# Column quarters for two modulation weights, and the order of slots and late units in a two-block kernel

## What is computed

```python
mod_x = (silu(c) @ w_mod + b_mod)          # 6 x 1024: sh1, sc1, g1, sh2, sc2, g2
mod_c = silu(c_ctx) @ w_mod + b_mod        # the same weights for a second vector
x   = x + g1x * (attention(...) @ w_out)
hx2 = rmsnorm(x) * (1 + sc2x) + sh2x
x   = x + g2x * peer(hx2)                  # g2x: the last two of twelve slices of w_mod

def peer(h):                               # rows in chunks of 128
    q = (h @ w_q).reshape(C, 8, 2, 128)
    s = einsum('chpd,hpnd->chpn', q, subkeys)
    sv, si = top_k(s, 16)                  # 16 per half; then 16 of the 256 pairs: ids
    a = gelu(einsum('cd,chkd->chk', h, u[ids]))
    return einsum('chk,chkd->cd', softmax(best) * a, v[ids])
```

## Time and profile before

| | us |
|---|---|
| median of 3 runs (lowest, highest) | 1465.23 (1464.28, 1466.23) |
| the profiled execution | 1464.12 |
| its span, first to last instruction | 1462.2 |
| busy PE, DVE, ACT, POOL | 1324.0, 1108.5, 629.8, 318.4 |
| gathers (268.45 of 416.32 MB) | share of 16 DMA engines 44.4% |
| mean granted clock of PE | 0.967 |

### The profile page before, as it was taken

How to read it: one execution, slowest core, us unless ns; L and a number is a source line. 1 busy time by engine, 2 the same in 40 slices (tenths; PEclk the granted TensorE clock), 3 DMA queues, 4 the chain that set the end, 5 groups by cost and what they waited for, 6 DMA issues and landing times.

```text
span 1462.2 us, 16525 instructions
## 1 busy us (share of the span) xinstructions
PE 1324.0 (91%) x5512; PEld 874.0 (60%) x5512; DVE 1108.5 (76%) x2315; ACT 629.8 (43%) x1322; POOL 318.4 (22%) x307
## 2 busy tenths in 40 slices
PE   9998899998797978697897799999999999999998
PEld 3876664543343424253343346678888877788887
DVE  6688857867776776766677777879998577799974
ACT  5343733223221222222221225567776445677752
POOL 0000003544444444344444430000110000011100
PEclk9999999999898989899898899999999999999999
DMA  9624457999999999999999996434545434345530
GB/s 392 270 116 192 160 248 308 421 422 422 420 422 421 422 422 420 422 417 421 418 421 410 413 413 264 171 118 156 190 173 198 156 117 166 115 179 198 199 144 30
DMA packets 50437, 416.32 MB, mean 285 GB/s; under 512 B 5552, under 2 KB 5680, under 8 KB 7088
## 3 DMA queue, kind: packets, MB, share of 16 engines
q0 software_dynamic: 36864, 268.45, 44.4%
q1 hardware_dynamic: 13488, 146.82, 26.3%
HBM read 414.20 MB, written 1.05 MB: 284 GB/s over the span
## 4 chain that ended last, share of the span: by engine, by line
DVE 38%; PE 35%; DMA 15%; issue 6%; ACT 3%; POOL 2%; DVEq 0%; SPq 0%; POOLq 0%; ACTq 0%
DVE arena_r L592 8%; DMA ring<-in_uv,ids 8%; PE ps L1199 6%; DMA arena<-in_uv,ids 6%; DVE ring L2237 4%; PE ps L1278 4%; PE ps L1280 4%; PE ps L1279 4%; DVE arena L2513 4%; DVE arena L2237 3%; DVE arena L2505 2%; DVE arena L2515 2%; PE ps L1018 2%; PE ps L907 2%; PE ps L909 2%
## 5 line engine op out<-in xcount | busy, mean ns | idle before, releaser
L1199 PE MATMUL ps<-ring,arena 128*128 128x512 f32 x632 | 295.2, 617 | 52.2 <-ACT arena L1714 52.2
L2237 DVE CUSTOM_DVE_ANT_0 ring<-ring,arena 128x1024 f32<-128x1024 f32 x158 | 190.5, 1224 | 88.6 <-DMA ring<-in_uv,ids 88.0
L1199 PEld LDWEIGHTS ps<-ring,arena 128*128 128x128 f32 x632 | 122.4, 197 | 215.0 <-issue 142.3
L1486 PE MATMUL ps<-hpair,arena_r 128*128 128x512 f32 x704 | 244.3, 394 | 0.0
L793 POOL DMA_INDIRECT ring<-in_uv,ids x158 | 177.9, 1126 | 228.1 <-PE ps L1199 176.2
L1199 PE MATMUL ps<-arena 128*128 128x512 f32 x392 | 186.1, 621 | 45.0 <-ACT arena L1714 45.0
L592 DVE TENSOR_TENSOR arena_r<-ring,arena_r 128x1024 fp32r<-128x1024 f32 x152 | 185.4, 1223 | 54.3 <-ACT arena_r L577 50.6
L1488 PE MATMUL ps<-hpair,arena_r 128*128 128x256 f32 x704 | 195.0, 277 | 0.0
L577 ACT ACTIVATE arena_r<-ring 128x1024 fp32r<-128x1024 f32 x152 | 158.7, 1053 | 59.0 <-PE ps L1280 58.0
L793 POOL DMA_INDIRECT arena<-in_uv,ids x98 | 105.1, 1072 | 350.5 <-issue 247.8
L1199 PEld LDWEIGHTS ps<-arena 128*128 128x128 f32 x392 | 76.7, 199 | 147.1 <-issue 91.1
(11 more groups left out here) (337 smaller groups left out, 2048.7 us busy)
## 6 DMA issues: line engine op xcount, KB each, us to landing
ring<-in_lw SPq DMA_DIRECT2D x39, 2048.0 KB, 7.9
ring<-in_b1w SPq DMA_DIRECT2D x14, 2048.0 KB, 8.8
ring<-in_b1w SPq DMA_DIRECT2D x9, 1024.0 KB, 16.8
ring<-in_lw SPq DMA_DIRECT2D x8, 1024.0 KB, 5.0
wqb<-in_wq SPq DMA_DIRECT2D x4, 1024.0 KB, 9.0
arena<-in_wq SPq DMA_DIRECT2D x3, 1024.0 KB, 13.5
ring<-in_uv,ids POOLq DMA_INDIRECT x158
ring<-in_lw SPq DMA_DIRECT2D x2, 1088.0 KB, 10.0
```

The lines of the kernel that those rows point to most:

```text
L1199: last = nc.tensor.matmul(ps[:, 4 + 2 * c + b, :], diag[:, k % 4, :], vrows[place(n, k)][:, b * 512:(b + 1) * 512], start=False, stop=(clo ...
L1486: nc.tensor.matmul(ps[:, bank, :].rearrange("p (t n) -> p t n", t=2), high_of(l, p)[:, cols_], hpair[:, :, k, :], start=(k == 0), stop=Fal ...
L2237: V.tensor_tensor_reduce(out=urows[at], in0=urows[at], in1=hrow[:, c, :], scale=1.0, scalar=0.0, op0=ALU.mult, op1=ALU.add, accum_out=dots ...
```

## The change

The last two modulation weights use four column quarters of the array: `sil32` holds the two silu columns and 30 zero columns, product k goes to partitions 32(k mod 4) on, and the eight products become two in each quarter. The copy out takes 128 rows, and `mod_cols` adds the quarters by multiplying with `sum4` (identity of two, repeated). Both weights move on PE from behind the output sums to behind the second key sums of chunk 0 (in place of two steps of `out_sums`, which are spread), and so do their copies on ACT and their bias on DVE. In the attention, turn(15), values(14) and values(15) go behind all output sums of unit 15; values(15) writes into another bank. On ACT, act_pt(15) goes before act_rows(14), and `roots(1, 4)` before the third `heads_in`. Gathers begin with slots 11, 12, 4, 5, 6, 7, 3, 0, 1, 2, 13, 14, 15, and the order changes by swaps of neighbours from round to round until it is the old one; the last nine gathers have their old slots.

```diff
--- before
+++ after
@@ -40,6 +40,7 @@
...
 MOD_A = 4
+MOD_ROWS = 32
 MODA_ORDER = (0, 2, 1, 3)
...
@@ -90,15 +91,37 @@
...
+FIRST_SLOTS = (11, 12, 4, 5, 6, 7, 3, 0, 1, 2, 13, 14, 15)
+def slot_order(count):
+    now, order = list(FIRST_SLOTS), []
+    while len(order) < count:
+        order += now
+        for i in range(len(order) // len(SLOTS) % 2, len(SLOTS) - 1, 2):
+            if SLOTS.index(now[i]) > SLOTS.index(now[i + 1]):
+                now[i], now[i + 1] = now[i + 1], now[i]
+    return order[:count]
+ORDER = slot_order(TOPK * STAGES)
+LAST_USE, TURN, USED_UP_TO = {}, [], []
+for g, at in enumerate(ORDER):
+    TURN.append(ORDER[:g + 1].count(at))
+    USED_UP_TO.append(LAST_USE.get(at, 0))
+    LAST_USE[at] = g + 1
+assert tuple(ORDER[-9:]) == SLOTS[0:9]
 def place(n, k):
-    return SLOTS[(TOPK * n + k) % len(SLOTS)]
+    return ORDER[TOPK * n + k]
 def turn_of(n, k):
-    return (TOPK * n + k) // len(SLOTS) + 1
-LAST_USE = {at: g + 1 for g in range(TOPK * STAGES) for at in (SLOTS[g % len(SLOTS)],)}
+    return TURN[TOPK * n + k]
 ENDS = tuple(GROUP * (g + 1) for g in range(GROUPS))
...
@@ -126,6 +149,7 @@
...
 TURN_BANK = 4
+LAST_VALUES = 3
 MODB_UNIT = (0, 2, 6, 9, 12)
...
@@ -297,6 +321,7 @@
...
         sil2 = small(8, 4)
+        sil32 = rot[:, 0:2, :].rearrange("p a b -> p (a b)").rearrange("p (k m) -> p k m", k=KD)
         modc = small(48, 2)
...
@@ -450,7 +475,7 @@
...
             if i >= MOD_A + MOD_B:
-                return modrow_c[0:2, :]
+                return modrow_c
             return modrow[0:4, i % 2, :]
...
@@ -662,7 +687,7 @@
...
             act.wait_ge(pv_done, m + 1)
-            src = ps[:, 6, 256 * (m % 2):256 * (m % 2) + P]
+            src = ps[:, LAST_VALUES if m == 15 else 6, 256 * (m % 2):256 * (m % 2) + P]
             if t < DIFF:
...
@@ -783,6 +808,7 @@
...
             nc.gpsimd.memset(sil2[:, :, 2:4], 0.0).then_inc(fills, 1)
+            nc.gpsimd.memset(sil32[:, :, 2:MOD_ROWS], 0.0).then_inc(fills, 1)
             nc.gpsimd.memset(zero, 0.0).then_inc(fills, 1)
...
@@ -800,8 +826,8 @@
...
                     pool.wait_ge(ids_ready, 1)
-                if k >= len(SLOTS):
-                    pool.wait_ge(pair_free, NS + k - len(SLOTS) + 1)
+                if USED_UP_TO[k]:
+                    pool.wait_ge(pair_free, NS + USED_UP_TO[k])
                 elif at == 3:
...
@@ -815,7 +841,7 @@
...
                 for k in range(TOPK):
-                    pool.wait_ge(pair_free, NS + TOPK * n + k - len(SLOTS) + 1)
+                    pool.wait_ge(pair_free, NS + USED_UP_TO[TOPK * n + k])
                     gather(n, n % NC, k)
...
@@ -839,8 +865,9 @@
...
                 for k in range(KD):
-                    last = nc.tensor.matmul(ps[0:2, bank, :], sil2[:, k, 0:2], slot(n)[:, k, :],
-                                            start=(k == 0), stop=(k == KD - 1))
+                    rows = slice((k % 4) * MOD_ROWS, (k % 4 + 1) * MOD_ROWS)
+                    last = nc.tensor.matmul(ps[rows, bank, :], sil32[:, k, :], slot(n)[:, k, :],
+                                            start=(k < 4), stop=(k >= 4), skip_group_check=True)
                 last.then_inc(mod_used, 1)
...
@@ -848,7 +875,7 @@
...
                     last = nc.tensor.matmul(ps[:, bank, at + 2 * jj:at + 2 * jj + 2], mod_row(i)[:, jj * P:(jj + 1) * P],
-                                            con("sum4")[0:4, :] if i < MOD_A else ident[0:2, 0:2], start=True, stop=True)
+                                            con("sum4")[0:4 if i < MOD_A else P, :], start=True, stop=True)
                 last.then_inc(modcol_done, 1)
...
@@ -911,7 +938,7 @@
...
-            pe.wait_ge(fills, 3)
+            pe.wait_ge(fills, 4)
             running(3, 8)
...
@@ -993,7 +1020,7 @@
...
                     for kc in range(4):
-                        last = nc.tensor.matmul(ps[:, 6, at:at + P], PT[:, m % 2, 0, kc * P:(kc + 1) * P],
+                        last = nc.tensor.matmul(ps[:, LAST_VALUES if m == 15 else 6, at:at + P], PT[:, m % 2, 0, kc * P:(kc + 1) * P],
                                                 vrow[:, kc, t * P:(t + 1) * P], start=(kc == 0), stop=(kc == 3))
...
@@ -1030,8 +1057,9 @@
...
                     scores(m + 2)
-                turn(m)
-                if m >= 1:
+                if m < 15:
+                    turn(m)
+                if 1 <= m < 15:
                     values(m - 1)
...
@@ -1058,12 +1086,10 @@
...
                     out_sums(1, 5, 4, 5, 6, 7)
+            turn(15)
+            values(14)
             values(15)
             turned(1, range(4, KD), 4)
-            pe.wait_ge(exp_done, 32)
-            pe.wait_ge(o_out, 3)
-            out_sums(0, 2, 0, 1)
...
@@ -1134,11 +1160,21 @@
...
             first_query(1, 7, range(3, KD)).then_inc(first_q, 1)
-            out_sums(0, 2, 2)
+            pe.wait_ge(exp_done, 32)
+            pe.wait_ge(o_out, 3)
+            out_sums(0, 2, 0)
             first_keys(1, 5)
-            out_sums(0, 2, 3)
+            out_sums(0, 2, 1)
+            pe.wait_ge(silu_ready, 2)
+            mod_rows(MOD_A + MOD_B, 6)
             back_to_rows(0, (0, 7))
-            out_sums(1, 3, 0, 1, 2, 3)
+            mod_rows(MOD_A + MOD_B + 1, 4)
+            out_sums(0, 2, 2, 3)
+            pe.wait_ge(row_out, 2)
+            mod_cols(MOD_A + MOD_B, 7)
+            out_sums(1, 3, 0, 1)
+            mod_cols(MOD_A + MOD_B + 1, 7, 8)
+            out_sums(1, 3, 2, 3)
...
@@ -1148,7 +1184,6 @@
...
             out_sums(1, 3, 4, 5, 6, 7)
-            mod_rows(MOD_A + MOD_B, 6)
             norm2_tiles(1, (0, 2))
...
@@ -1156,9 +1191,6 @@
...
             back_to_rows(1, (0, 2))
-            pe.wait_ge(row_out, 2)
-            mod_cols(MOD_A + MOD_B, 7)
-            mod_rows(MOD_A + MOD_B + 1, 6)
...
@@ -1204,11 +1236,10 @@
...
             all_queries(1)
-            mod_cols(MOD_A + MOD_B + 1, 3)
             experts(0, 0, places=range(GROUP, 2 * GROUP))
...
             experts(0, 0, places=range(2 * GROUP, TOPK))
-            pe.wait_ge(mod_out, MOD_A + MOD_B + 1)
+            pe.wait_ge(mod_out, MODS)
             cleared(6, 7)
...
@@ -1536,7 +1567,7 @@
...
                     act.wait_ge(modcol_done, i - 1)
-                nc.scalar.activation(mod_row(i), ps[0:4 if i < MOD_A else 2, bank, :], ACT.Copy).then_inc(modrow_out, 1)
+                nc.scalar.activation(mod_row(i), ps[0:4 if i < MOD_A else P, bank, :], ACT.Copy).then_inc(modrow_out, 1)
...
@@ -1643,11 +1674,10 @@
...
             table(ACT.Sqrt)
+            act_pt(act, 15)
             act_rows(act, 14)
-            act_pt(act, 15)
             act_rows(act, 15)
+            roots(1, 4)
             heads_in(3, range(4, KD), 4)
...
@@ -1678,19 +1708,19 @@
...
-            roots(1, 4)
             norm2_in(0)
...
                 nc.scalar.activation(qTs[:, s, 0:P], ps[:, bank, 0:P], ACT.Copy).then_inc(first_q_out, 1)
+            mod_row_out(MOD_A + MOD_B, 6)
             rows_in(0, (0, 7))
+            mod_row_out(MOD_A + MOD_B + 1, 4)
             heads_in(4, range(4), 0, con("subg"))
...
             table(ACT.Gelu)
-            mod_row_out(MOD_A + MOD_B, 6)
             norm2_in(1)
...
@@ -1717,7 +1747,6 @@
...
             table(ACT.Gelu)
-            mod_row_out(MOD_A + MOD_B + 1, 6)
             query_out(1)
...
@@ -1937,6 +1966,7 @@
...
             V.tensor_copy(sil4[:, :, 0:2], sil2[:, :, 0:2]).then_inc(sil4_ready, 1)
+            V.tensor_copy(sil32[:, :, 0:2], sil2[:, :, 0:2]).then_inc(silu_ready, 1)
             dve.wait_ge(sil4_ready, 1)
...
@@ -2261,13 +2291,14 @@
...
             topk(1, 0, 1)
+            dve.wait_ge(modcol_done, MODS)
             mod_bias(MOD_A + MOD_B, 7)
+            mod_bias(MOD_A + MOD_B + 1, 7, 8)
             for k in range(GROUP, TOPK):
...
             weights(0, 0, 3, ENDS)
-            mod_bias(MOD_A + MOD_B + 1, 3)
             dve.wait_ge(row_out, 4)
...
```

## The result

| | before | after |
|---|---|---|
| median, us (lowest, highest; 22 runs each, side by side) | 1466.45 (1464.28, 1471.43) | 1469.28 (1466.47, 1474.09) |
| ratio, 95% interval | | 1.0020 [1.0014, 1.0027] |
| the profiled execution, us | 1464.12 | 1472.42 |
| its span, us | 1462.2 | 1470.6 |
| last gather issued, us | 861.45 | 866.8 |

The change makes the kernel 2.8 us (0.2%) slower. The forecast was 2.5 us faster, and 1469.28 lies above its range. Up to the first load of the second block (880.15 before, 885.53 after) they are 5.4 us apart; the other 3.0 lie in the second block, which the change does not touch: there the mean of 704 products of one line is 399 ns instead of 394.

What follows compares the result with a forecast made beforehand. Bound by the expert gather stream: 1.3 us from an earlier start plus 1.4 to 2.4 of start loss is 2.7 to 3.7, capped at the 18th gather, so 2.5 us taken: 1462.7 us, range 1460.2 to 1466.5.

Steps and rivals of the forecast that it cites:

- Bound by the gather stream: 256 expert gathers run at the DMA ceiling, 410 to 422 GB/s; only their start, start loss and dry spells count.
- Part 1, late unit: Late attention unit: turn(15) and values(14) go behind the output sums, so everything to the first indices comes 1.33 us sooner.
- rival D: Does nothing: PE's clock falls in the new 1.7 us wait, or slot order or chunk 1 takes the gain; 0.11.
- Part 2, column quarters: Modulation weights on PE: four quarters overlap, 1.9 to 2.2 us a weight instead of 7.03.
- Rivals B and C: Quarters overlap in pairs only, 1464.2 us, chance 0.12; or don't overlap, 1471 us, chance 0.09.
- Part 3, the new order: PE's list: last output sum 236.3, 6.0 us later; chunk 1 turned 3.6 us later, PE's loss repaid behind its indices.
- The 18th gather gains 0.7 to 1.7 us, no more.: Release of the 18th gather: fourth dot ends at 265 to 266, instead of the gelu of 266.98.
- Part 4, gathers: Gather start: six go out at once, nothing runs dry, start loss falls from 3.3 to 0.9 to 1.9 us.
- the cushion of 1.6 us: Data still unmoved when the 18th gather's can begin in the kernel before: 0.68 MB, 1.6 us from dry.
- the 22 early reuses: Cases reusing a slot after 12 gathers instead of 13; 45th and 61st singled out, cost 0, at worst 2 us.
- Rival E: Slower: chunk 1 makes the 18th gather 2 us later and the stream dry there; 3 us lost, 1468.2 us; 0.06.
- The cap by the cushion: At the 18th gather: cushion 1.6 plus 0.7 to 1.7 us sooner limits the gain to 2.3 to 3.3 us.

Runs made afterwards that it cites:

- e1: The changed kernel unaltered, run and profiled a second time: 1471.49 us, ratio 1.0024 to before.
- e5: Changed kernel with both mod_cols and the cleared banks behind the last output sums, ScalarE's second copy ahead of roots(1, 6): 1465.10 us, ratio 0.9989.
- e11: Changed kernel with the slot order's first round of swaps left out: 1470.43 us, ratio 1.0017.
- e6: Changed kernel with idle products in three TensorE waits, the third behind all_queries(1): 1467.01 us, ratio 1.0004.
- e2: Changed kernel with idle products in TensorE's first two waits (3 and 10): 1468.48 us, ratio 1.0002.
- e8: e5 with idle products in TensorE's first wait (3) and in the one behind all_queries(1) (5): 1464.65 us, ratio 0.9988.
- e4: Kernel before with the column quarters alone, every step left in its place: 1466.84 us, ratio 0.9999.
- e3: Changed kernel with both mod_cols and the cleared banks behind the last output sums, ScalarE's second copy behind roots(1, 6): 1471.19 us, ratio 1.0020.
- e9: e5 with the gathers' slots in their old, cyclic order: 1470.97 us, ratio 1.0023.
- e12: e5 with the slot order's first round of swaps left out: 1466.76 us, ratio 0.9992.
- e10: e5 with eight idle products on TensorE ahead of the last output sums' second halves: 1470.03 us, ratio 1.0022.

## Why the prediction was wrong, point by point

**Bound by the gather stream**: right. The lead or lag of the stream at 300 us, from the windows, gives each version's difference in time to before within some 2 us.

**Part 1, late unit**: predicted -1.33 us. DVE's first residual is 1.71 us sooner than before (200.01 against 201.72), and the first gather 1.0 sooner after and 1.8 in e1. The difference is the clock fall in the new wait of 1.66 us, rival D's mechanism, which happened in one of two executions of the changed kernel: e5's first residual starts at 200.00 too, its clock held, and its first gather goes at 222.86 instead of 223.59. The residual itself varies, from 199.94 in e1 to 200.88 in e11, so the 1.33 us are right within that.

**Part 2, column quarters**: predicted 1.9 to 2.2 us; 1.92. The next instruction starts 1.86 us after the first record (216.69 to 218.55), so four slots of 0.43 and 0.14 for entering and leaving the mode. Rivals B and C fall. By the figure of the Trainium skill (TensorE: Matmul & The Clock Gate, Part 3) for three column tiles the estimate was 2.2 for four; the trace has 7.03/1.92, a speedup of 3.66, and the measurement decides.

**Part 3, the new order**: the places were right where the clock held. Last output sum predicted 236.3; 236.15 in e1, 237.65 after. Chunk 1 turned predicted 240.8; 240.77 in e1, 242.27 after. PE's wait predicted 4.6; 4.62. Queries done predicted 246 to 248; 247.8 in e1, 249.5 after. **The step that failed is the next one**: "The 18th gather gains 0.7 to 1.7 us, no more." It lost 1.7 in e1 and 3.2 after. The terms of that step that were wrong:

- The indices of chunk 1 were put at 260.3 to 261.3; they came at 263.52 after, and at 261.75 in e1.
- From the fourth dot on the sum took over the 3.7 us of before (266.98 to 270.71). After, it is 5.5 (268.41 to 273.89): the weights stand behind the fifth dot (0.8 us more), and PE works at the half clock behind the wait of 2.96 us (0.9 more: 3.70 us from its restart to the gather, before 2.79). In e1 this term alone makes the loss: its fourth dot ended at 266.6, 0.6 us later than predicted but still ahead of the gelu of before (266.98), and from there it is 5.8 us. I had written that PE's loss is repaid, because a mod_cols and 7 us of products no longer stand there. True, but these had been the cover of that wait (0.49 us before). **Work taken off an engine leaves a wait behind, and the question of what the clock does in it was asked for the first wait and the second, not for this one.** e6 shows its price, 1.5 us at the 18th gather (2.8 us from restart to issue, e2 4.3).
- The lateness was to be caught up because PE was the last to arrive. After the change DVE's indices and dots are, and they carry the whole lateness of chunk 1.

**Part 4, gathers**: the start was right, and better than taken: 226 to 240 at 408 GB/s, a loss of 0.4 us where I left 0.9 to 1.9. That makes the other end worse: the data are used up sooner (at about 272, against 274.0 by the cushion of 1.6 us) and the 18th gather comes later. An estimate from these: data used up 2 us sooner and a gather 3.2 us later, less the 1.6 us of cushion, make 3.6 us without data, and that is what 272 to 276 lack (2x(396+372)/421 = 3.6). The other 2.4 us of the hole are the refill and the 19th gather, which I had among the 22 early reuses but not among those that matter. Slot 13 was counted as not dry with an issue by 249; after, it goes at 250.34 and the 14th gather at 255.98, and 240 to 262 loses 1.1 us; in e1 (420 GB/s) nothing.

**Rival E** had the right mechanism and the right size (1468.2, 3 us lost; it decides once the 18th gather is 1.1 us later than today) and got 0.06. Against it stood one argument, that `all_queries(1)` goes forward. That the three causes listed for it push in one direction and have a common origin, PE's list ahead of the last output sums, was reason enough for more. The cap by the cushion was written into the forecast as an upper bound of the gain; it was as well the point from which the sign turns.

What stays open: the share of the late unit alone; how much of what e5 loses behind 300 (1.3 of 2.8 us) is the slot order's and how much the fast execution of before; and why TensorE's clock falls in one execution and holds in the next.

## What to carry to other kernels

A transfer stream with a small cushion at one issue converts each microsecond of lateness there into about a microsecond of time (2.6 us into 2.4, e6 against e8), and earliness into nothing (e4); so work moved ahead of the critical release has to be priced at the next issue that is near dry, and a faster start has already spent that cushion. When an instruction is moved or made shorter, list every wait that it used to cover and ask for each what TensorE's clock does in it. Put only what frees a buffer ahead of the release (here the two weights), and what merely uses the result (mod_cols, cleared banks) into the wait behind it, with its ScalarE copy ahead of the chain that the wait is for.

## What the runs showed of the hardware

- Four column quarters overlap fully for fp32 products of 128x32 by 512: 16 records in 1.92 us against 7.03 in one tile, in each execution looked at.
- The fall of TensorE's clock is not a function of the program alone. After a wait of 1.65 to 1.66 us the granted clock fell from 2.4 to 1.2 GHz in one execution and held in another of the same kernel (22 records 4.43 and 2.80 us); of the eight profiled executions with this wait unfilled it fell in that one (after) and held in seven (e1, e3, e5, e9 to e12). After 2.95 to 2.97 us it held in e5 (16 records 7.13 us) and was low in the seven others (after, e1, e2, e3, e10, e11, e12; 8.65 to 10.06 us), e12 with the same TensorE list as e5. After 4.62 us it was low in both executions of the changed kernel.
- Eight idle products of 128x256 (16 records) take 3.62 us in e10. Three and ten of them in the first two waits kept the granted clock at 1.00 in e2 (222 to 266), and five more in the third kept it at 1.00 in e6 from 205 to 290.
- Gathers of 1.05 MB each: from an empty queue, the first 14 us (226 to 240) ran at 323 GB/s with two gathers ready and the next 5.2 us behind them, at 382 to 408 with six ready, and at 217 with two ready and the third 10.3 us behind them (e9).
